# Two decoder layers on one core: gate rows folded by DMA, spatial weights transposed by the host, the mLSTM denominator as a 257th column

## The reference

```python
y = mix(x @ w_in) @ w_out ;  x = layer_norm(alpha * x + y)
# A: dilated window attention, 8 heads of 64, three (window, dilation) groups
# B: spatial gating
w = w_s * tril(ones(128, 128))
mixed = einsum('gts,bcsgk->bctgk', w, vc) + b_s ;  sgu = u * mixed
# C: mLSTM, 4 heads of 256, chunks of 128; ig = input gate, lf = log sigmoid(forget gate)
b = cumsum(lf) ;  D = b[t] - b[s] + ig[s] (causal) ;  m = max_s D
sc = (q @ k.T) * exp(D - m) ;  num = sc @ v ;  den = sc.sum(-1)
h = num / max(|den|, exp(-m))
```

## Time and profile before

| | before |
|---|---|
| median of 3 runs | 1353.81 us (1352.55 to 1355.03) |
| the profiled execution: its time | 1353.17 us |
| the profiled execution: its span | 1351.4 us |
| PE busy | 1337.6 us (99%) |
| PEld, DVE, ACT, POOL busy | 1105.1, 800.0, 640.6, 189.1 us |

### The profile page before, as it was taken

One profiled execution on the slowest core, in us unless ns is written; L12 is line 12 of the kernel. 1 busy time (PEld: TensorE's weight loads), 2 busy tenths in 40 slices (PEclk: granted clock), 3 DMA queues, 4 the chain that ended last, 5 costly groups with the idle time before them and its releaser, 6 DMA issues.

```text
span 1351.4 us, 16310 instructions
## 1 busy us (share of the span) xinstructions
PE 1337.6 (99%) x6400; PEld 1105.1 (82%) x6400; DVE 800.0 (59%) x1192; ACT 640.6 (47%) x899; POOL 189.1 (14%) x239
## 2 busy tenths in 40 slices
PE   9999999999999999999999999999999999999997
PEld 8888888888888888888888888888888888888885
DVE  5655555545657664765775555555546576648656
ACT  5454344345455553444563544454445555434442
POOL 0410310410312000300003121121121200004000
PEclk9999999999999999999999999999999999999998
DMA  9864664664466665476666546646635655654662
GB/s 326 266 181 129 186 178 134 187 174 139 127 186 188 190 190 180 125 231 192 212 192 197 171 129 192 178 127 188 179 115 166 191 173 180 194 167 149 217 206 103
DMA packets 126461, 240.91 MB, mean 178 GB/s; under 512 B 12000, under 2 KB 12048, under 8 KB 125872
## 3 DMA queue, kind: packets, MB, share of 16 engines
q1 hardware_dynamic: 123360, 230.85, 57.1%
q0 software_dynamic: 1664, 6.92, 1.4%
q10 hardware_dynamic: 1360, 2.10, 0.4%
HBM read 237.74 MB, written 2.10 MB: 177 GB/s over the span
## 4 chain that ended last, share of the span: by engine, by line
PE 92%; DVE 3%; ACT 2%; DMA 2%; issue 0%; SPq 0%; DVEq 0%; ACTq 0%
PE ps L325 83%; DMA w_raw<-w_in_dram 2%; DVE w_lo L924 1%; PE ps L462 1%; ACT w_hi L667 1%; PE ps L436 1%; PE ps L594 1%; ACT arena L731 1%; PE ps L473 1%; PE ps L477 1%; PE ps L475 1%; PE ps L451 1%; PE ps L449 1%; PE ps L519 1%; PE ps L343 1%; PE ps L562 1%
## 5 line engine op out<-in xcount | busy, mean ns | idle before, releaser
L924 DVE TENSOR_TENSOR w_lo<-w_raw,w_hi 128x1024 fp32r<-128x1024 f32 x408 | 529.3, 1303 | 471.2 <-ACT w_hi L667 470.6
L667 ACT ACTIVATE w_hi<-w_raw 128x1024 fp32r<-128x1024 f32 x408 | 429.6, 1058 | 522.6 <-PE ps L325 494.4
L325 PE MATMUL ps<-w_hi,xT_hi 128*128 128x512 f32 x1632 | 649.1, 398 | 0.1
L325 PE MATMUL ps<-w_hi,xT_lo 128*128 128x512 f32 x1632 | 638.0, 391 | 0.0
L325 PE MATMUL ps<-w_lo,xT_hi 128*128 128x512 f32 x1632 | 636.2, 390 | 0.0
L325 PEld LDWEIGHTS ps<-w_hi,xT_lo 128*128 128x128 f32 x1632 | 306.9, 188 | 65.9
L325 PEld LDWEIGHTS ps<-w_hi,xT_hi 128*128 128x128 f32 x1632 | 307.2, 188 | 65.2 <-issue 4.0
L325 PEld LDWEIGHTS ps<-w_lo,xT_hi 128*128 128x128 f32 x1632 | 307.6, 188 | 61.1
L731 ACT ACTIVATE arena<-arena,nmax 128x128 f32<-128x128 f32 x96 | 42.5, 444 | 39.2 <-DVE nmax L1023 39.2
L256 POOL TENSOR_TENSOR carried<-sel 1x1 f32<-1x1 f32 x18 | 10.2, 566 | 353.8 <-DVE arena L1166 178.7
L325 PE MATMUL ps<-ahead,xT_hi 128*128 128x512 f32 x184 | 57.1, 392 | 0.0
(11 more groups left out here) (223 smaller groups left out, 907.7 us busy)
## 6 DMA issues: line engine op xcount, KB each, us to landing
w_raw<-w_in_dram SPq DMA_DIRECT2D x368, 512.0 KB, 3.8
w_raw<-w_out_dram SPq DMA_DIRECT2D x64, 512.0 KB, 4.9
mix<-x_t_dram SPq DMA_DIRECT2D x8, 256.0 KB, 6.0
xres<-x_dram ACTq DMA_DIRECT2D x4, 512.0 KB, 11.4
z<-ln_g_dram POOLq DMA_DIRECT2D x2, 1024.0 KB, 6.5
store<-ln_b_dram POOLq DMA_DIRECT2D x2, 1024.0 KB, 7.5
out_dram<-xres SPq DMA_DIRECT2D x4, 512.0 KB, 2.9
hg<-head_g_dram POOLq DMA_DIRECT2D x4, 256.0 KB, 6.2
```

Source lines behind the costliest of these rows:

```text
L325: mm = pe.matmul(ps[2 * s + t][:], a[:, order[c] * KC + k, t * P:(t + 1) * P], b[:, k], start=(c + k + i == 0), stop=(c == CH - 1 and k == ...
L667: A(hi_of(n, c), w_raw[:, c % RING], ACT.Copy).then_inc(w_hi_done, 1)
L924: TTn(lo_of(n, c), w_raw[:, c % RING], hi_of(n, c).bitcast(F32), ALU.subtract).then_inc(w_lo_done, 1)
```

## The change

1. The gate rows: `fold` is gone. ACT issues three DMAs that copy rows 4 to 15 of `gprod` onto partitions 0 to 3 (`gpart`), and DVE adds them to the bias and the first rows.
2. The maximum: `sel` is gone. ACT issues a DMA of `gmax` (4 KB) to DRAM, and later one that brings it back to all 128 partitions (`gbc`, 512 KB). DVE reads `gbc` in SBUF where it read PSUM.
3. PE turns `ga` and `gem` into columns three chunks later, inside block N_SV, and DVE makes `decay` two splits and a copy later, ACT its exponential one split later.
4. The host gives the spatial weights transposed, and they are loaded into `wspT`.
5. `vM` gets a 257th column of ones in each head, and the products with the values give the denominator beside the numerator. The 12 one-column matmuls are gone. A head's output now takes two PSUM banks, and banks 4 and 5 serve the odd heads. DVE works out the denominator head by head inside `head_output`.
6. The matmuls at the start: 9 on the identity, then 10 on a zeroed tile of the rounded type with 64 to 256 columns, then 6 that use 64 rows of the array.

```diff
-        vM = arena[:, 4096:6144].rearrange("p (t c) -> p t c", t=TT)
-        scE = arena[:, 6144:7680].rearrange("p (h s) -> p h s", h=MH)
+        vM = arena[:, 4096:4096 + TT * MH * (MD + 1)].rearrange("p (t h c) -> p t h c", t=TT, h=MH)
+        scE = arena[:, 6152:7688].rearrange("p (h s) -> p h s", h=MH)
...
-        fold = sb("fold", [2 * NG, NG])
+        gpart = z[0:MH, 1].rearrange("p t c -> p (t c)")[:, 0:3 * SEQ].rearrange("p (i t) -> p i t", i=3)
+        gbc = z[:, 1].rearrange("p t (h c) -> p (t h) c", c=SEQ)
+        gmax_dram = nc.dram_tensor("gmax_dram", (DEPTH, MH, SEQ), F32, kind="Internal").ap()
...
-            for _ in range(20):
+            for _ in range(9):
                 pe.matmul(ps[7][:, 0:P], ident[:], ident[:], start=True, stop=True)
+            pe.wait_ge(gw_zero, 1)
+            for n in (64, 64, 64, 64, P, P, P, P, 2 * P, 2 * P):
+                pe.matmul(ps[7][:, 0:n], gw[:, 0:P], gw[:, P:P + n], start=True, stop=True)
+            for _ in range(3):
+                for h in range(2):
+                    rows = slice(HD * h, HD * (h + 1))
+                    pe.matmul(ps[5 + h][:, 0:P], gw[rows, 0:P], gw[rows, P:2 * P], start=True, stop=True)
...
-                chunks(N_SU, Q_SU, 0, 0, 2)
-                pe.wait_ge(params, (l + 1) * 16 * N_PARAMS)
-                pe.wait_ge(z_act, taken_act(l, Q_GATES))
-                pe.wait_ge(og_act, (l + 1) * (GROUPS * PAIRS) + 1)
-                pe.wait_ge(og_dve, (l + 1) * (GROUPS * PAIRS) + 1)
-                for s in range(SG):
-                    tr = pe.transpose(ps[7][:, s * P:(s + 1) * P], wsp[:, s, :], ident[:])
-                tr.then_inc(wsp_ps, 1)
-
-                for a in range(2):
-                    mm = pe.matmul(ps[6][0:MH, a * SEQ:(a + 1) * SEQ], fold[:, a * MH:(a + 1) * MH], gprod,
-                                   start=True, stop=True)
-                mm.then_inc(g_ps, 1)
-                chunks(N_SU, Q_SU, 0, 2, 8)
+                chunks(N_SU, Q_SU, 0, 0, CH)
+                chunks(N_SV, Q_SV, 1, 0, 3)
                 pe.wait_ge(g_dve, l * 2 + 2)
                 pe.wait_ge(g_act, l * 2 + 2)
-                pe.wait_ge(wsp_copied, l + 1)
-
-                for h in range(MH):
-                    pe.matmul(ps[4 + h // 2][:, (h % 2) * SEQ:(h % 2 + 1) * SEQ], sel[:, h, :], gmax,
-                              start=True, stop=True)
+                pe.wait_ge(og_dve, (l + 1) * (GROUPS * PAIRS) + 1)
...
-                chunks(N_SV, Q_SV, 1, 0, CH)
+                chunks(N_SV, Q_SV, 1, 3, CH)
...
-
                 pe.wait_ge(msc_done, (l + 1) * MH)
-                for h in range(MH):
-                    pe.matmul(ps[4][:, h:h + 1], scE[:, h, 0:P], ones[:], start=True, stop=True)
-                    pe.matmul(ps[4][:, MH + h:MH + h + 1], scE[:, h, P:2 * P], ones[:], start=True, stop=False)
-                    mm = pe.matmul(ps[4][:, MH + h:MH + h + 1], scE[:, h, 2 * P:3 * P], ones[:],
-                                   start=False, stop=True)
-                mm.then_inc(mden_ps, 1)
...
-                    o, v = ps[6 + h % 2], slice(h * MD, (h + 1) * MD)
-                    pe.matmul(o[:, 0:MD], scE[:, h, 0:P], vM[:, 0, v], start=True, stop=True)
-                    pe.matmul(o[:, MD:2 * MD], scE[:, h, P:2 * P], vM[:, 0, v], start=True, stop=False)
-                    mm = pe.matmul(o[:, MD:2 * MD], scE[:, h, 2 * P:3 * P], vM[:, 1, v],
+                    o = 6 - 2 * (h % 2)
+                    pe.matmul(ps[o][:, 0:MD + 1], scE[:, h, 0:P], vM[:, 0, h, :], start=True, stop=True)
+                    pe.matmul(ps[o + 1][:, 0:MD + 1], scE[:, h, P:2 * P], vM[:, 0, h, :], start=True, stop=False)
+                    mm = pe.matmul(ps[o + 1][:, 0:MD + 1], scE[:, h, 2 * P:3 * P], vM[:, 1, h, :],
...
-                transposes(mix, CH, OUT_ORDER, 0, ((mden_done, l + 1), (mix_att, l + 1)))
+                transposes(mix, CH, OUT_ORDER, 0, ((h_done, (l + 1) * MH), (mix_att, l + 1)))
...
-                    A(dst, ps[2 * s][:], ACT.Copy).then_inc(z_act, 1)
+                    src = ps[2 * s][:]
+                    if len(dst.shape) == 3:
+                        src = src.rearrange("p (h d) -> p h d", d=MD)
+                    A(dst, src, ACT.Copy).then_inc(z_act, 1)
...
+                act.wait_ge(z_act, taken_act(l, Q_GATES))
+                for i in range(3):
+                    act.dma_start(gpart[:, i], z[(i + 1) * MH:(i + 2) * MH, 0, 0, 0:SEQ]).then_inc(gpart_landed, 16)
...
+                act.dma_start(gmax_dram[l], gmax).then_inc(gmax_stored, 16)
                 A(gem[:], gm, ACT.Exp, scale=-1.0).then_inc(g_act, 1)
-                split(N_SV, 1, 4)
+                split(N_SV, 1, 2)
+                act.wait_ge(gmax_stored, (l + 1) * 16)
+                act.dma_start(gbc, gmax_dram[l].rearrange("h t -> (h t)").partition_broadcast(P).rearrange("p (h t) -> p h t", h=MH)
+                              ).then_inc(gbc_landed, 16)
+                split(N_SV, 2, 4)
                 take(N_SV, 0, su[:, 0, :])
-                split(N_SV, 4, 5)
+                split(N_SV, 4, 6)
                 act.wait_ge(decay_dve, l + 1)
                 A(decay[:], decay[:], ACT.Exp, scale=-1.0).then_inc(decay_act, 1)
-                split(N_SV, 5, 8)
+                split(N_SV, 6, 8)
...
-                take(n, 0, vM[:, 0, 0:BW])
+                take(n, 0, vM[:, 0, 0:2, 0:MD])
                 split(n, 4, 8)
                 split(N_MG1, 0, 4)
-                take(N_MG1, 1, vM[:, 0, BW:2 * BW])
+                take(N_MG1, 1, vM[:, 0, 2:4, 0:MD])
...
-                dve.wait_ge(g_ps, l + 1)
+                dve.wait_ge(gpart_landed, (l + 1) * 3 * 16)
                 carry_dve()
-                for a in range(2):
-                    f = TS(grow[:, a, :], ps[6][0:MH, a * SEQ:(a + 1) * SEQ], gbias[:, a:a + 1], None, ALU.add)
+                for a, (hi, lo) in enumerate(((gprod[0:MH], gpart[:, 1]), (gpart[:, 0], gpart[:, 2]))):
+                    f = STT(grow[:, a, :], hi, gbias[:, a:a + 1], lo, ALU.add, ALU.add)
...
-                dve.wait_ge(wsp_ps, l + 1)
-                V.tensor_copy(wspT[:], ps[7][:].rearrange("p (s t) -> p s t", s=SG)).then_inc(wsp_copied, 1)
...
-                split(N_SV, 0, 3)
+                split(N_SV, 0, 4)
+                take(N_SV, 0, su[:, 1, :])
+                split(N_SV, 4, 5)
+                dve.wait_ge(gbc_landed, (l + 1) * 16)
...
-                    src = ps[4 + h // 2][:, (h % 2) * SEQ:(h % 2 + 1) * SEQ]
-                    TS(decay[:, h, 0:SEQ], src, gcol[:, 0, 0, h:h + 1], 0.0, ALU.subtract, ALU.max)
-                    f = TS(decay[:, h, SEQ:3 * P], src[:, P:SEQ], gcol[:, 0, 1, h:h + 1], 0.0,
+                    TS(decay[:, h, 0:SEQ], gbc[:, h, :], gcol[:, 0, 0, h:h + 1], 0.0, ALU.subtract, ALU.max)
+                    f = TS(decay[:, h, SEQ:3 * P], gbc[:, h, P:SEQ], gcol[:, 0, 1, h:h + 1], 0.0,
                            ALU.subtract, ALU.max)
                 f.then_inc(decay_dve, 1)
-                split(N_SV, 3, 4)
-                take(N_SV, 0, su[:, 1, :])
-                split(N_SV, 4, 8)
+                split(N_SV, 5, 8)
...
-                take(n, 0, vM[:, 1, 0:BW])
+                V.memset(vM[:, :, :, MD:MD + 1], 1.0)
+                take(n, 0, vM[:, 1, 0:2, 0:MD])
...
+                    o = 6 - 2 * (h % 2)
                     for t in range(TT):
-                        f = STT(at(t), ps[6 + h % 2][:, t * MD:(t + 1) * MD], den[:, 1, t, h:h + 1], at(t),
+                        f = TTn(den[:, 0, t, h:h + 1], ps[o + t][:, MD:MD + 1], gcol[:, 1, t, h:h + 1], ALU.max)
+                    own(f)
+                    for t in range(TT):
+                        f = STT(den[:, 0, t, h:h + 1], ps[o + t][:, MD:MD + 1], -1.0, den[:, 0, t, h:h + 1],
+                                ALU.mult, ALU.max)
+                    own(f)
+                    V.reciprocal(den[:, 1, :, h], den[:, 0, :, h]).then_inc(den_done, 1)
+                    dve.wait_ge(den_done, l * MH + h + 1)
+                    for t in range(TT):
+                        f = STT(at(t), ps[o + t][:, 0:MD], den[:, 1, t, h:h + 1], at(t),
...
-                take(N_MG1, 1, vM[:, 1, BW:2 * BW])
+                take(N_MG1, 1, vM[:, 1, 2:4, 0:MD])
                 split(N_MG1, 4, 5)
 
-                dve.wait_ge(mden_ps, l + 1)
-                sums = ps[4][:, 0:TT * MH].rearrange("p (t h) -> p t h", t=TT)
-                own(TS(den[:, 0], sums, -1.0, None, ALU.mult))
-                own(TTn(den[:, 0], sums, den[:, 0], ALU.max))
-                own(TTn(den[:, 2], den[:, 0], gcol[:, 1], ALU.max))
-                f = V.reciprocal(den[:, 1], den[:, 2])
-                f.then_inc(mden_done, 1)
-                dve.wait_ge(mden_done, l + 1)
...
-                load(wsp[:], w_spatial[l])
+                load(wspT[:], w_spatial[l])
...
-        "w_spatial": np.transpose(w_spatial, (0, 2, 1, 3)),
+        "w_spatial": np.transpose(w_spatial, (0, 3, 1, 2)),
```

(7 more changed lines are left out.)

21 lines of the change are left out of this document (8 added, 13 removed).

## The result

The kernel after takes 1339.94 us (median of 4 runs, 1337.33 to 1341.91), the kernel before beside it on the same chip 1353.18 (1351.63 to 1355.03). The ratio is 0.9892, with a 95% interval of 0.9875 to 0.9909: faster by 13.2 us. The forecast was 1338.3, in a range from 1336.5 to 1343.6.

A forecast was written before the change was run, and what follows sets the result against it. PE was taken to bound the kernel, with DVE, ACT and weight loads running ahead. Removed rows and half clock, 15.46 us, from 1353.17 gave 1337.7 profiled; plus 0.64 for the median, 1338.3, range 1336.5 to 1343.6.

The forecast's parts named there:

- The sum: Both layers' rows removed from PE plus the half clock behind the one-column matmuls: 15.46 us less.
- the transposes, the folding and the spreading: Gate-stage rows leaving PE: 1.59 us a layer for spatial weights and folding, 1.83 for spreading `gmax`.
- the one-column rows with the clock behind them: Before the values: rows of 2.69 us a layer go, and half clock behind them, 1.61 and 1.63 us.
- this dip goes with its cause: At the values: the half clock goes with the stretch where PE is full of rows but feeds almost no columns.
- The rival that the clock dips anyway: At the four heads' products between chunks: the half clock stays, 3.24 us comes back, 1341.5 us; 10%.
- The 257th column: Products with the values, 24 rows a layer: the added column costs 0.04 us, taken as nothing.
- Its rival, 0.11 a row: Products with the values: each added column costs a one-column row, 5.3 us comes back, 1343.6 us; 4%.
- The start: Shorter warm-up on PE: could gain 0 to 1.05 us, taken as nothing because PE waits for DVE near 41 us.
- a longer wait there: Sign: at 41 us PE's wait for DVE would be longer than before.
- the cold first chunk: First chunk after the new warm-up at half clock: 2.73 us more, 1.05 given back, +1.7, 1340.0 us; 7%.
- The two thinnest margins: Gate stage: 0.7 us of slack for `gbc` before PE wants chunk 5; none for chunk 2's split behind the store.
- the rival that ends slower: Both transfers of the maximum take 11.4 us: 9.1 lost a layer, 1356.5 us; decides near 22 us after `gm`; 2%.

The follow-up runs named there:

- e3: Kernel before with the gate DMAs, the maximum by DMA and host-transposed spatial weights; no 257th column, old start: 1346.65 us, ratio 0.9945.
- e2: Kernel before with the spatial weights transposed by the host alone; folding, `sel` and the one-column matmuls stay: 1356.92 us, ratio 1.0011.
- e1: Kernel before with the 257th value column and nothing else: 1346.52 us, ratio 0.9949.
- e6: e2 with 64 columns of ones instead of one in the denominator matmuls: 1353.39 us, ratio 0.9994; 3.5 us under e2.
- e8: e7 with the load of `gbc` issued a second time and DVE waiting for the second: 1351.38 us, ratio 0.9983.
- e4: Kernel before with the new matmuls at the start only: 1355.92 us, ratio 1.0012.
- f4: Kernel before with the four loads of x issued in the second attention group instead of near 21 us: 1352.72 us, ratio 0.9986.
- f1: Kernel after, unchanged, run again beside the last kernels: 1339.22 us, ratio 0.9883.
- e5: Kernel after with the 20 old matmuls at the start: 1340.46 us, ratio 0.9892.
- e7: Kernel after with the load of `gbc` issued behind the splits of chunks 2 to 5 of N_SV instead of ahead of them: 1341.63 us, ratio 0.9904.

## Why the prediction was right

**The sum.** The forecast was 15.46 for the rows and the clock together; the rest fell by 15.28, and in four more traces with the same program behind the start by 15.16 to 15.29. Of its parts, e3 gives 6.8 for the transposes, the folding and the spreading (forecast 6.84), e2 0.8 for the transposes alone, and e1 8.4 for the one-column rows with the clock behind them (8.62). The half clock behind them is 3.2 for both layers by e6 (3.24).

**The clock.** The step "this dip goes with its cause" held, and e6 ties the dip to the single column: it came behind one-column rows at 8 of 10 places, behind the same rows with 64 columns at none of 2, with PE busy in both. The rival that the clock dips anyway fell: in after no dip is left at the values. The Trainium skill, "TensorE: Matmul & The Clock Gate", the table "Why this matters for your kernels", lets idle gaps between bursts bring the throttle back; e8 and e4 agree (half clock behind a wait of 5.3 us, and behind one of 2.5), but before the dips at the values no gap stands, so the page's rule is not the only way down.

What the prediction had too certain: a dip is not in every execution. e3 and f4 keep the one-column rows and show one dip instead of two, and e1 and e2 show one behind the spreading of `gmax`, where before has none. The medians contain a mixture of this, the profile one draw. So part of the gain in the median is that dips behind `sel` can no longer happen, which no term of the sum has, and part of the 3.24 was not there in every run of before. The granted clock over whole runs says how the two come out together: it is 0.9950 in the mean of 64 runs of before (0.993 to 0.997) and 0.9975 in the four of after, and 0.0025 of 1351 us is 3.4 us (an estimate), about the 3.24 of the sum. The medians fell by 13.2 beside after and by 14.95 beside f1; what is missing to the sum should then lie in the start.

**The 257th column** at nothing: 0.43 a product, as before. Its rival, 0.11 a row, fell.

**The start** at nothing: near on the average (e4 1.0012, e5 the ratio of after), but the reason given for it did not hold. The prediction said that whatever PE gains at its start it waits longer near 41 us, and named a longer wait there as a sign. In the trace of after the wait is shorter than before, 0.2 against 0.3: DVE's splits came earlier too (39.30 against 39.81), and 0.52 of the earlier start is still there at the anchor. In other executions the start costs time: there is the stall near 41 us (2.65, and 1.70 of clock behind it, in e4), and there is the cold first chunk, which the prediction had as a rival with 7%, at +1.7 us. It is real and dearer: the chunk takes 2.4 more (forecast 2.73), but the prediction let the earlier start give back 1.05, where in f1 the chunk starts 0.59 later than before; at the anchor this makes +2.7. The two runs of after near 1341.8 and the two near 1337.8 may be a cold chunk or a stall, since e5, with the old start, has two runs near 1341.9 as well; only the fastest of after's four has a trace, so this is open. The median is 1.6 above the forecast, well inside the range, and 2.6 above the profiled execution, for which the sum was made.

**The transfers.** Here too a number was off, though it cost nothing. The prediction took 6.5 us for the store of 4 KB and called the slack behind it thin. The timeline of ACT's queue, kernel after:

```profile
358.10 0.31 ACTq L788 DMA_DIRECT2D gmax_dram<-conv_y  x1
...
359.38 0.37 ACTq L792 DMA_DIRECT2D z<-gmax_dram  x1
```

The second DMA waits for the store to land, and it is issued 1.28 after the first. So the store took at most 1.3, not 6.5. The load of `gbc` takes 5.4 by the page's list of DMA issues:

```profile
z<-gmax_dram ACTq DMA_DIRECT2D x2, 512.0 KB, 5.4
```

It lands at about 364.8, where the prediction had 371.7; DVE cannot use it before 370.16. The two thinnest margins were 0.7 and 0. For the first, `gbc` was there more than 5 us before DVE could use it, and by e7 and e8 DVE could start 2.2 later still before PE noticed, where the prediction had 1.7: so that part of the reckoning was sound, and only the transfers were taken too long. For the second, ACT's issue waited only until 359.38, and the splits behind it lost nothing. The mechanism of the rival that ends slower was right, its decision point is not: it was put at a landing 22 us after `gm` is ready, and in e8 one 19.6 us after the store's issue (359.31 to 378.9) gives back the whole gain of the rest, because the half clock behind a wait had no term in it.

**DVE.** `decay` reads `gbc` in SBUF instead of PSUM, and its eight rows take 1.84 us from 370.37 to 372.21 instead of 2.61. A head's denominator takes 0.70 (533.47 to 534.17), as forecast.

## What to carry to other kernels

A stretch of matmuls with one column costs twice: by its rows, 0.11 us each here whether they had 1 or 64 columns, and by the half clock behind it, which is only seen in the starts of the matmuls that follow; give such products a column in a matmul that runs anyway. When a stall is moved off an engine by a DMA, measure the slack by delaying the DMA on purpose: past it a microsecond of delay cost PE a microsecond here, and the half clock behind the wait came on top (4.7 us on 10.8). And where runs of one kernel scatter, compare traces from an anchor behind the part that scatters, then look at that part for itself: here loads that nobody needed before the end of the layer delayed the first weights.
